# Expert outputs accumulated by the scatter in a 512-row buffer, the last expert's rows and the down biases summed in PSUM

## The reference, cut to what matters

```
x = x + hybrid_mixer(rms_norm(x, norm_mix_g), w_in, w_out, pos)
h = rms_norm(x, norm_ffn_g)
logits = h @ w_router + b_router
top_val, top_idx = top_k(logits, 4);  gates = softmax(top_val)
for each token t and each of its 4 experts e:
    gu  = h[t] @ w_gate_up[e] + b_gate_up[e]
    act = min(gu[:1024], 7) * sigmoid(1.702 * min(gu[:1024], 7)) * (clip(gu[1024:], -7, 7) + 1)
    x[t] += gate * (act @ w_down[e] + b_down[e])
out = rms_norm(x, norm_final_g)
```

## Time and profile before

| | |
|---|---|
| median of 3 runs | 1566.33 us (1566.11 to 1566.35) |
| the profiled execution, its own time | 1565.52 us |
| its span in the profile | 1563.7 us |
| PE busy over the span | 1449.2 us, 93% |
| DVE / ACT / POOL busy | 1248.9 / 979.9 / 597.5 us |
| DMA | 458.19 MB, 293 GB/s in the mean |

### The profile page before, as it was taken

How to read it: one execution, slowest core, us unless ns; L and a number is a source line. 1 busy time by engine, 2 the same in 40 slices (tenths; PEclk the granted TensorE clock), 3 DMA queues, 4 the chain that set the end, 5 groups by cost and what they waited for, 6 DMA issues and landing times.

```text
span 1563.7 us, 20137 instructions
## 1 busy us (share of the span) xinstructions
PE 1449.2 (93%) x6760; PEld 1188.6 (76%) x6760; DVE 1248.9 (80%) x1013; ACT 979.9 (63%) x719; POOL 597.5 (38%) x419
## 2 busy tenths in 40 slices
PE   6989999778999999999999999999999999999950
PEld 5877877666888888888888888888888888888840
DVE  5444545467989898888998989988898888988968
ACT  5243232355777777777777777777777777777721
POOL 0000000323444554555544544444444444445522
PEclk9999998879999999999999999999999999999975
DMA  8211332267999999999999999999999999999925
GB/s 304 81 55 55 110 104 73 89 233 286 366 354 356 361 360 361 360 361 359 362 361 357 358 352 361 358 358 354 360 357 365 361 360 360 362 357 362 332 86 208
DMA packets 128697, 458.19 MB, mean 293 GB/s; under 512 B 13456, under 2 KB 13472, under 8 KB 127456
## 3 DMA queue, kind: packets, MB, share of 16 engines
q1 hardware_dynamic: 116832, 436.23, 77.6%
q0 software_dynamic: 10128, 18.79, 3.3%
q10 hardware_dynamic: 1712, 2.84, 0.6%
HBM read 454.14 MB, written 21.50 MB: 304 GB/s over the span
## 4 chain that ended last, share of the span: by engine, by line
PE 71%; DMA 11%; issue 7%; DVE 5%; ACT 3%; POOLq 2%; POOL 1%; ACTq 0%; SPq 0%; DVEq 0%
PE ps L1520 17%; PE ps L1521 16%; PE ps L1526 16%; DMA xg<-h_rows,idx_gather 10%; PE ps L1254 4%; PE ps L1260 4%; PE ps L1255 4%; PE ps L1498 2%; PE ps L1507 2%; PE ps L1512 1%; POOLq L514 1%; ACT actT_hi L751 1%; DVE wlo L849 1%; POOL tab L515 1%; ACT whi L618 1%
## 5 line engine op out<-in xcount | busy, mean ns | idle before, releaser
L849 DVE TENSOR_TENSOR wlo<-raw,whi 128x2048 fp32r<-128x2048 f32 x274 | 621.8, 2288 | 146.3 <-ACT whi L618 146.3
L618 ACT ACTIVATE whi<-raw 128x2048 fp32r<-128x2048 f32 x274 | 525.1, 1916 | 199.6 <-PE ps L1526 160.8
L1520 PE MATMUL ps<-whi,xT_hi 128*128 128x512 f32 x1024 | 406.5, 397 | 0.0
L1521 PE MATMUL ps<-whi,xT_lo 128*128 128x512 f32 x1024 | 402.4, 393 | 0.0
L1526 PE MATMUL ps<-wlo,xT_hi 128*128 128x512 f32 x1024 | 276.5, 392 | 0.0
L507 POOL TENSOR_SCALAR has<-slots,pair 128x128 fp32r<-128x128 f32 x128 | 181.0, 1424 | 127.3 <-issue 127.3
L1526 PEld LDWEIGHTS ps<-wlo,xT_hi 128*128 128x128 f32 x1024 | 192.9, 188 | 42.9
L1521 PEld LDWEIGHTS ps<-whi,xT_lo 128*128 128x128 f32 x1024 | 193.4, 189 | 42.1
L1520 PEld LDWEIGHTS ps<-whi,xT_hi 128*128 128x128 f32 x1024 | 193.4, 189 | 41.9
L1520 PE MATMUL ps<-whi,actT_hi 128*128 128x512 f32 x512 | 204.6, 400 | 4.7 <-issue 4.7
L1521 PE MATMUL ps<-whi,actT_lo 128*128 128x512 f32 x512 | 201.5, 394 | 0.0
(11 more groups left out here) (207 smaller groups left out, 1667.1 us busy)
## 6 DMA issues: line engine op xcount, KB each, us to landing
raw<-in_w_gate_up SPq DMA_DIRECT2D x130, 1024.0 KB, 6.9
raw<-in_w_down SPq DMA_DIRECT2D x126, 1024.0 KB, 7.3
raw_a<-in_w_gate_up SPq DMA_DIRECT2D x63, 1024.0 KB, 6.6
raw_b<-in_w_gate_up SPq DMA_DIRECT2D x63, 1024.0 KB, 6.7
raw<-in_w_in SPq DMA_DIRECT2D x14, 1024.0 KB, 5.4
picked<-y_rows SPq DMA_DIRECT2D x8, 1024.0 KB, 13.5
raw<-in_w_out SPq DMA_DIRECT2D x4, 1024.0 KB, 4.9
x<-in_x SPq DMA_DIRECT2D x4, 512.0 KB, 8.2
```

Of the source, the lines that this page charges most:

```text
L618: nc.scalar.activation(whi_slot(n), raw_slot(slot_of(n)), ACT.Copy).then_inc(hi_done, 1)
L849: nc.vector.tensor_tensor(wlo_slot(n), raw_slot(slot_of(n)), whi_slot(n).bitcast(F32), ALU.subtract).then_inc(lo_done, 1)
L1520: mm(ps[:, bank + half, :], x_hi_t[:, k0 + k, :], w_hi_ap, start=k0 + k == 0 and not started, stop=False)
L1521: mm(ps[:, bank + half, :], x_lo_t[:, k0 + k, :], w_hi_ap, start=False, stop=False)
```

## The change

The scatter no longer writes one row for each pair but adds to 512 rows, `acc_rows`, which SP fills with `x1` before. All but the last expert go that way, and SP loads the 512 rows back into `x1` (four DMAs of 512 KB) when scatter number 32 (the empty one and experts 0 to 30) has landed. The last expert's rows are not scattered. `has`, its slot matrix, is transposed on PE; its `y` is split into `y_hi` (ACT) and `y_lo` (DVE), and three products for each chunk (gates x down biases, `hasT` x `y_hi`, `hasT` x `y_lo`) add up in PSUM. One DVE addition puts them onto `x1`. The destination row goes: `pairs` has four columns instead of five, and L1047 to L1052 are gone. The overflow lists are built before the loop, over 128 partitions, and two DMAs issued by ACT bring them onto one partition. The final gain is multiplied in together with the scale. A square root ahead of the last down product has ACT's table loaded early.

```diff
@@ SP
                 if n == U_MOE + RAW_E:
+                    for c in range(NC):
+                        sp.wait_ge(x1_s, NC + c + 1)
+                        sp.dma_start(acc_rows[c * P:(c + 1) * P, :], x1[:, c, :]).then_inc(x1_out, 16)
                     for c in range(NC):
                         sp.wait_ge(hn_s, c + 1)
@@ SP, after the last weights
-            sp.wait_ge(ov_s, 1)
+            sp.wait_ge(scattered, 16 * E)
+            for c in range(NC):
+                sp.dma_start(x1[:, c, :], acc_rows[c * P:(c + 1) * P, :]).then_inc(x_back[c], 16)
+            sp.wait_ge(ov_s, 32)
...
-            sp.wait_ge(rows_done, 1)
-            for c in range(NC):
-                for k in range(0, TOPK, 2):
-                    sp.dma_start(picked[c][:, k:k + 2, :], y_view[c][:, k:k + 2, :]).then_inc(picked_in[2 * c + k // 2], 16)
@@ POOL
-                pl.indirect_dma_start(out=y_rows, out_offset=bass.IndirectOffsetOnAxis(ap=idx_scatter[:, 0:1], axis=0),
+                pl.indirect_dma_start(out=acc_rows, out_offset=bass.IndirectOffsetOnAxis(ap=idx_scatter[:, 0:1], axis=0),
                                       in_=source, in_offset=None,
-                                      bounds_check=S * TOPK - 1, oob_is_err=False).then_inc(done, 16)
+                                      bounds_check=S - 1, oob_is_err=False, compute_op=ALU.add).then_inc(done, 16)
...
+            pl.wait_ge(x1_out, 16 * NC)
...
-            scatter(expert_rows(E - 1), scattered)
-            pl.wait_ge(scattered, 16 * (E + 1))
...
-            for c in range(NC):
-                pl.wait_ge(picked_in[2 * c], 16)
-                nc.gpsimd.tensor_tensor(picked[c][:, 0, :], picked[c][:, 0, :], picked[c][:, 1, :], ALU.add).then_inc(f_pair, 1)
@@ ACT, before the loop
+            act_e.wait_ge(ov_num, 1)
+                for k in range(2):
+                    act_e.dma_start(ov_lists[0:1, k, :], ov_int[0:16, k:k + 1]).then_inc(ov_s, 16)
@@ ACT, after the loop
-            gated_rows(E - 1, 16 * E, U_ALL)
+            act_e.wait_ge(has_tr, 1)
+            nc.scalar.activation(hasT[:, :], ps[:, 1, :], ACT.Copy).then_inc(hasT_s, 1)
+            nc.scalar.activation(small[:, 12, 0:1], cst[:, C_ONE:C_ONE + 1], ACT.Sqrt)
+            act_e.wait_ge(used, U_ALL)
+            nc.scalar.activation(y_hi[:, :], ps[:, 4:6, :].rearrange("p b t -> p (b t)"), ACT.Copy,
+                                 scale=tab[:, E - 1, 1:2]).then_inc(yhi_s, 1)
@@ DVE, before the loop (moved here from the end, 16 x 2 reductions replaced by 2)
+            v.wait_ge(counts_s, 1)
...
+            nc.vector.tensor_copy(ov_int[:, :], ov_out[:, :]).then_inc(ov_num, 1)
@@ DVE, after the loop
+            v.wait_ge(yhi_s, 1)
+            nc.vector.scalar_tensor_tensor(out=y_lo[:, :], in0=ps[:, 4:6, :].rearrange("p b t -> p (b t)"),
+                                           scalar=tab[:, E - 1, 1:2], in1=y_hi[:, :].bitcast(F32), op0=ALU.mult,
+                                           op1=ALU.subtract).then_inc(ylo_s, 1)
...
             def final_sum(c):
-                link(nc.vector.tensor_tensor(x1[:, c, :], x1[:, c, :], t[:, 0, :], ALU.add))
-                link(nc.vector.tensor_tensor(t[:, 2, :], t[:, 2, :], t[:, 3, :], ALU.add))
-                nc.vector.tensor_tensor(x1[:, c, :], x1[:, c, :], t[:, 2, :], ALU.add).then_inc(f_sum, 1)
-                nc.vector.tensor_tensor(t[:, 0, :], x1[:, c, :], gain_row[:, :], ALU.mult).then_inc(f_gain, 1)
+                v.wait_ge(x_back[c], 16)
+                v.wait_ge(f_ps, c + 1)
+                nc.vector.tensor_tensor(x1[:, c, :], x1[:, c, :], ps[:, LAST_BANK[c]:LAST_BANK[c] + 2, :]..., ALU.add).then_inc(f_sum, 1)
 
             def final_norm(c):
-                nc.vector.tensor_scalar(picked[c][:, 0, :], picked[c][:, 0, :], small[:, 3, c:c + 1], None,
-                                        ALU.mult).then_inc(f_out, 1)
+                nc.vector.scalar_tensor_tensor(out=x1[:, c, :], in0=x1[:, c, :], scalar=small[:, 3, c:c + 1], in1=gain_row[:, :],
+                                               op0=ALU.mult, op1=ALU.mult).then_inc(f_out, 1)
@@ PE, after the loop (transposes ahead of down, the rest behind it)
+            pe.wait_ge(has_s, E + 2)
+            for c in range(NC):
+                last = nc.tensor.transpose(ps[:, 1, c * P:(c + 1) * P], has[:, c, :].bitcast(F32), ident)
             down(U_ALL - U_DN, E - 1)
-            for c in range(NC):
-                for half in range(2):
-                    last = mm(ps[:, GB_BANK[c] + half, :], gateT[:, c * P:(c + 1) * P], bdn[:, half * UW:(half + 1) * UW],
...
+            for c in range(NC - 1):
+                last_rows(c, gateT, bdn, True, False)
+            pe.wait_ge(yhi_s, 1)
+            for c in range(NC - 1):
+                last_rows(c, hasT, y_hi, False, False)
+            pe.wait_ge(ylo_s, 1)
+            for c in range(NC - 1):
+                last_rows(c, hasT, y_lo, False, True).then_inc(f_ps, 1)
+            last_rows(NC - 1, ...)
```

More of the change, by code:

```diff
@@ L253, in build @@
     ovr, o = place(o, "ovr", [3 * E])
-    ov_out, o = place(o, "ov_out", [2, 16])
+    ov_eq, o = place(o, "ov_eq", [3 * E])
+    ovt, o = place(o, "ovt", [3 * E])
+    ov_out, o = place(o, "ov_out", [2])
+    ov_int, o = place(o, "ov_int", [2], I32)
     assert o <= area + 24 * K
@@ L278, in build @@
     actT32, _ = place(area + 56 * K, "actT32", [KD, P])
-    picked = [place(at, f"picked{c}", [TOPK, D])[0] for c, at in enumerate((area, area + 48 * K, base, base + 16 * K))]
+    hasT_over, o = place(area + 44 * K + 4 * P, "hasT_over", [S])
+    assert o <= area + 48 * K
+    hasT, o = place(area + 104 * K, "hasT", [S], F32R)
+    assert o <= nc.sbuf_usable_end, (o, nc.sbuf_usable_end)
+    y_hi, _ = place(area + 32 * K, "y_hi", [D], F32R)
+    y_lo, _ = place(area + 36 * K, "y_lo", [D], F32R)
     ps = nc.alloc_psum_tensor("ps", [P, 8, UW], F32)
@@ L514, in store_table @@
                 pl.drain()
-                nc.gpsimd.tensor_tensor(rows[:, 2:3], rows[:, 2:3], rows[:, 3:4], ALU.add).then_inc(done, 1)
+                nc.gpsimd.tensor_tensor(rows[:, 1:2], rows[:, 1:2], rows[:, 2:3], ALU.add).then_inc(done, 1)
             def expert_rows(e):
@@ L786, in _ @@
             tokens_hi(1)
+            act_e.wait_ge(ov_num, 1)
+            with nc.allow_non_contiguous_dma(reason="16 pairs of numbers onto one partition"):
+                for k in range(2):
+                    act_e.dma_start(ov_lists[0:1, k, :], ov_int[0:16, k:k + 1]).then_inc(ov_s, 16)
             with act_e.Fori(0, E - 1) as i:
@@ L1133, in _ @@
             activated(0)
+            v.wait_ge(counts_s, 1)
+            for k in range(3):
+                last = nc.vector.tensor_scalar(ovf[:, k * E:(k + 1) * E], counts[:, :], float(P * (k + 1)), None, ALU.is_gt)
+            link(last)
+            link(nc.vector.tensor_tensor_scan(out=ovr[:, :], data0=cst[:, C_ONE:C_ONE + 3 * E], data1=ovf[:, :],
+                                              initial=0.0, op0=ALU.mult, op1=ALU.add))
+            nc.vector.tensor_copy(ov_total[0:1, 0:1], ovr[0:1, 3 * E - 1:3 * E]).then_inc(total_s, 1)
+            v.wait_ge(total_s, 1)
+            link(nc.vector.tensor_tensor(ovr[:, :], ovr[:, :], ovf[:, :], ALU.mult))
+            link(nc.vector.tensor_scalar(ov_eq[:, :], ovr[:, :], cst[:, C_NUM:C_NUM + 1], None, ALU.is_equal))
+            for k, col in ((0, C_OVE), (1, C_OVC)):
+                link(nc.vector.tensor_tensor_reduce(out=ovt[:, :], in0=ov_eq[:, :], in1=cst[:, col:col + 3 * E],
+                                                    scale=1.0, scalar=0.0, op0=ALU.mult, op1=ALU.add,
+                                                    accum_out=ov_out[:, k:k + 1]))
+            nc.vector.tensor_copy(ov_int[:, :], ov_out[:, :]).then_inc(ov_num, 1)
             with v.Fori(0, E - 1) as i:
@@ L1609, in _ @@
                         for c in range(NC):
+                            last = nc.tensor.transpose(ps[:, 2, c * P:(c + 1) * P], has[:, c, :].bitcast(F32), ident)
+                        last.then_inc(v_htr, 1)
+                        for c in range(NC):
                             last = mm(ps[:, 3, 0:4], has[:, c, :], pair[:, c, 0:4], start=(c == 0), stop=(c == NC - 1))
```

167 lines of the change are left out of this document (78 added, 89 removed).

## The result

The changed kernel takes **1617.34 us** (median of 4 runs, 1607.89 to 1631.61), the kernel before 1566.34 on the same chip: ratio 1.0331, 95% interval 1.0292 to 1.0371. It is slower by 3.3%. The prediction said 1534, 2.1% faster, and held 1530 to 1546.

The account below looks back on a forecast made before the run. PE's pace was taken to bound the loop, a chain of small steps the end. Span 1563.7 - 31.4 (end) - 0.9 (before the loop), loop 0, gave 1531.4, hence a median of 1534 us; range 1530 to 1546.

Parts of the forecast that it names:

- The loop, forecast at 0: Trips of the expert loop: the adding scatter was taken to cost 0, bounds -4 and +37 us.
- the two covers: In the loop: 2.6 us for POOL's longer scatter issue, 5.2 us for the scatter's later landing before the gather's hand-over.
- Rival B: Loop: the scatter's part behind the issue doubles (6.4 us more), the gather's data waits; +37 us, or 1571; chance 0.07.
- The end, forecast -31.4: After the last down matmul: 12.4 us less until the first addition and 19.0 less behind it.
- the first sum: At the end: DVE's first addition was to come about 3.3 us after the last down matmul.
- PE's branch: At the end: PE's load of the overflow number, releases and branch, taken as off the path; 0, bound 2.0 us.
- The rows were back: At the end: accumulated rows loaded by 1512.6, 1.4 us before the first sum at 1514.0; cost 0, bound +5.
- From chunk to chunk: At the end on DVE: scaling of chunks 1 and 2 starts 3.7 us after the one before.
- The table load of ACT ... leave: At the end: ACT's table load and POOL's work were to leave, so neither was counted in the sum.
- C's other parts: The end shrinks less: PE's branch +2.0, lower PE clock +3.5 or late rows +5 us; 1536 to 1545; chance 0.17.
- Before the loop, forecast -0.9: DVE's routing chain ahead of the loop loses three operations, 0.86 us; bounds -0.9 and 0.
- 0.55 and 0.17: Chances: 0.55 for loop unchanged and end as worked out (1530 to 1538), 0.17 for the end shrinking less.

Follow-up runs that it names:

- the fourth experiment: The kernel before with a POOL memset of 128x512 behind each scatter's issue and one drain behind the loop: 1565.74 us, ratio 0.9997.
- The tenth experiment: Changed kernel without drains, next gather ahead of the scatter, plus ScalarE's early root moved behind the overflow branch: 1537.30 us, ratio 0.9818.

## Why the prediction was wrong

**The loop, forecast at 0, measured +69.1 us.** The step that failed is the one with the two covers. For POOL's issue it said "It may grow by 2.6 before the table's first step moves". It grew by 0.64 us, the first step did not move, and the fourth experiment shows this cover to be real. For the transfer it said "landing at 919.9 (9.2 us after 910.74), while POOL hands the gather over by 925.1: 5.2 us of cover". I measured the landing against the event that would matter if only the DMA queue tied the two transfers together, and took POOL as free once the scatter was issued. In fact the drain between the table's two steps ends 0.3 us after the landing, in the kernel before as in the changed one. The cover that the landing really had was the gap between two of DVE's subtractions: POOL's steps have to be through ahead of the one that starts at +11.2 (+11.3 in the changed kernel). From the changed kernel's trips, where landings up to +10.9 got in, I estimate that one up to about +10.7 would have cost nothing before. That is 1.5 us above the median of 9.2, and the adding took 1.8. In 20 of 30 trips POOL's steps were caught by DVE's subtraction and the gather went out 2 to 3 us later, into a chain of which the prediction itself says that a microsecond more in each trip costs up to 31 us. In the 10 slowest trips the gather's issue was held up as well (3.2 us), PE idled for 3.1 to 4.7 us, and in the one shown some 5.4 us of work at the lower clock followed. All this makes 2.3 us in a trip. The rows were at hand: the table's second step waits 3.0 us in a trip for "issue", 4.0 at most, where the instruction ahead of it had ended, and the listing has a drain there.

The Trainium skill (SBUF — State Buffer, "SBUF: two separate sides") says that DVE and GpSimd share one pair of ports under a lock: whichever starts first holds it for a whole instruction, and the other is blocked. For a DVE operation with two inputs in SBUF, as the subtraction is, it says so against a GpSimd operation that reads SBUF. The trace agrees: the second step takes 0.19 us, or, when it starts inside the subtraction of 2.29 us, until 0.05 to 0.17 us behind the subtraction's end (43 trips of the two kernels).

**Rival B** had the right sign and its first half (the adding scatter lands later, and the gather pays), but not its mechanism or size. It waited for a landing of 15.4 us, from which the gather's data would queue; the landing is 11.0, and what decides is POOL's drain and the gap between DVE's operations, which leaves some 1.5 us to use up instead of 5.2. The rule that it was weighed by (the Trainium skill, Collectives: The Full Stack, "The bandwidth ceiling: the fold count and why AG ≠ RS ≠ AR"), an add halving the rate, would have doubled the part behind the issue, 6.4 us more; measured was 1.8 us more in all, of which 0.6 is the issue.

**The end, forecast -31.4, measured -30.0.** The timeline of the changed kernel's end, which answers to the earlier trace rows:

```profile
1574.04 1.77 SPq L442 DMA_DIRECT2D x<-acc_rows  x4
1583.13 1.12 ACT L818 ACTIVATE y_hi<-ps,tab 128x1024 fp32r<-128x1024 f32 x1 [12.87 <-PE ps L1527]
1584.27 1.28 ACT L842 ACT_TABLE_LOAD   x1
1584.29 1.28 DVE L1181 SCALAR_TENSOR_TENSOR y_lo<-ps,tab,y_hi 128x1024 fp32r<-128x1024 f32 x1 [12.92 <-ACT y_hi L818]
1586.56 2.35 DVE L1218 TENSOR_TENSOR x<-x,ps 128x1024 f32<-128x1024 f32 x2 [0.99 <-PE ps L1643]
...
1588.98 1.28 ACT L845 ACT_TABLE_LOAD   x1
...
1590.58 0.16 DVE L865 RECIPROCAL small<-small 128x1 f32<-128x1 f32 x1 [1.43 <-ACT small L845]
...
1591.56 1.28 DVE L1229 SCALAR_TENSOR_TENSOR x<-x,small,gain_row 128x1024 f32<-128x1024 f32 x1
...
1595.34 1.28 DVE L1229 SCALAR_TENSOR_TENSOR x<-x,small,gain_row 128x1024 f32<-128x1024 f32 x1
```

- The last down matmul ends at 1583.10, and the first sum starts 3.46 us later; forecast was 3.3.
- PE's branch, taken at 0 with 2.0 as its bound, is 0: the bias products start at 1582.93, before the last down matmul is over.
- The rows were back: SP loads them from 1574.04 on, and the slowest of the four loads landed 7.1 us after an issue of 1575.4 at the latest, so by 1582.5, 4.1 us ahead of the sum.
- From chunk to chunk it is 3.78 us (1595.34 - 1591.56), forecast 3.7. From the first sum to the first scaling it is 5.0 us (1591.56 - 1586.56), forecast 4.1: this is the largest miss of the end, and the next point says whose it is.
- "The table load of ACT ... leave" was wrong. The early root loaded its table at 1568.77, and the squares still load one at 1584.27 and the root another at 1588.98; DVE waits 1.43 us for it. The tenth experiment shows it: with the early root behind the branch, only one load is left, and it is hidden. This is most of the 1.4 us.
- Of C's other parts none came: the bias products take 0.25 us each (1.52 for six, from 1582.93), and the granted clock is 1.00 from there to the last product, so it had not fallen.

The Trainium skill (ScalarE: Activation LUTs, "Table sets: the hidden batching unit") says that tables come in sets, and advises to group calls by set. The trace agrees that squares behind a root need no further load (none stands behind 1588.98), and it shows besides that the set loaded for the early root, ahead of the branch, was not the one in place for the squares behind it.

**Before the loop, forecast -0.9, measured +3.1 us.** From the end of the masks to ACT's copy of the first table's product it is 5.86 us instead of 6.72, so the routing gave the 0.86 us forecast. But at the residual, ahead of all that the change touches there, the changed kernel already stood 2.9 us later (ACT's conversion at 284.55 instead of 281.70), having drifted by 0.4 us at 30 us and 1.2 at 113. And between that copy (2.1 us later than before) and the first `y` (3.1 later) another 1.0 us went. It shows at PE's gap ahead of the loop: the products behind it had the lower granted clock for 3.4 us in the kernel before (358.6 to about 362) and for 5.9 in the changed one (360.2 to about 366.1). The versions that I made start their first `y` between 396.7 and 399.7 us. No edit of the experiments accounts for it; the cause is open.

**The chances.** 0.55 and 0.17 stood on a loop that was thought covered twice. One of the two covers was taken from the distance between two transfers and never checked against what POOL was seen to wait for. That the end came within 1.4 us was no luck: apart from the table load each of its parts is right within 0.2 us.

With the drains gone, what the change was worth is seen: 1538.12 against 1555.77 for the two kernels without drains, 17.7 us. Their spans differ by 16.7 us: 29.8 less at the end, 9.5 more in the 30 trips of slower PE, 2.6 more ahead of the first `y` and 1.0 more in the last trip.

## What to carry to other kernels

A wait that the profile puts down to "issue", behind an instruction that has ended, has a releaser that the profile can't name: compare its end with the landing of every DMA that the same engine has under way before a cover is counted. On GpSimd, order two of its own instructions by a semaphore that the first one raises; a drain in a loop with indirect DMAs makes every one of them synchronous, and what they take longer can then go onto the path. A step that comes later may also meet another engine's operation that it used to miss: here a landing after 11.1 instead of 10.9 us has the gather issued at +14.7 instead of +12.4. Where a chain has no cover, bound each thing that it touches by the event that it really waits for, and not by the one that comes last in the queue.

## What the hardware showed beyond that

- The instruction behind a drain on GpSimd starts 0.2 to 0.3 us after the landing of the indirect DMA issued ahead of the drain, 0.9 us where that instruction is itself an indirect DMA: in the changed kernel landings at 888.6 and 999.45 us and next starts at 888.88 and 999.72, in the kernel before 919.3 and 919.63, with the gather first 933.4 and 933.65 (and 921.1 and 922.03 for a scatter behind a gather).
- An adding scatter of 64 rows of 4 KB in the mean, beside weights at some 340 to 360 GB/s, issues for 3.51 us instead of 2.96 and lands after 11.0 instead of 9.2. Where nothing waits for it, the adding costs nothing that these runs can tell (1538.12 and 1537.06 us).
- The issue of the gather takes 1.1 us on POOL when it starts outside DVE's subtraction of 2.29 us; when it starts inside, it ends 0.94 to 0.99 us behind the subtraction's end: 2.5 to 2.7 us in all 30 trips before, 2.3 to 2.6 or 3.2 in 20 of 30 after, 1.1 in the other 10. I had read the 2.65 us of the earlier trace rows as a fixed price. It is not the drain that sets it; without drains the gather goes out at +8.4, where DVE's subtraction isn't yet there (it starts at +8.6), and lands 7.4 us later instead of 8.9.
- In a gap of 3.3 us on PE (1009.3 to 1012.6) the granted clock fell to 0.50 and stayed there for some 5.4 us of work behind it; the products stood 0.43 us apart instead of 0.23.
